# Fused decay-and-add of the samples' recurrent states, a gate chunk loaded ahead, and gate products moved between their fill sites

## What is computed

```python
def step(S, blk):                       # HGRN2, one chunk
    ...
    S = S * jnp.exp(b_last)[..., None] + jnp.einsum(
        "bhsk,bhsv->bhkv", kc * jnp.exp(b_last[:, :, None] - b), vc)
    return S, o
...
merged = (jax.nn.sigmoid(gate_a) * (o_a.astype(x.dtype) @ w_branch_a)
          + jax.nn.sigmoid(gate_b) * (o_b.astype(x.dtype) @ w_branch_b))
```

## Time and profile before

| | before |
|---|---|
| runs (3) | 1315.21, 1316.23, 1316.17 us; median 1316.17 |
| the profiled execution: its time | 1315.27 us |
| the profiled execution: its span | 1313.5 us |
| PE busy | 1284.6 us, 98% of the span |
| DVE, ACT, POOL busy | 28%, 18%, 4% |
| DMA | 449.40 MB, mean 342 GB/s |

### The profile page before, as it was taken

The page is one execution under the profiler, slowest core; times in us unless marked ns, Lnnn a source line. Parts: engine busy times, 40 slices in busy tenths (PEclk is TensorE's granted clock), DMA queues, the critical chain, the costliest instruction groups (busy, mean ns, idle before and its releaser), DMA issues.

```text
span 1313.5 us, 18378 instructions
## 1 busy us (share of the span) xinstructions
PE 1284.6 (98%) x7361; PEld 614.0 (47%) x7361; DVE 372.6 (28%) x1016; ACT 241.7 (18%) x532; POOL 56.6 (4%) x131
## 2 busy tenths in 40 slices
PE   9999999999999999999999999999999999999997
PEld 6778778888744333333333333333333333233333
DVE  3234756554327121121221211212112111211112
ACT  3144343222122110111111110111101101110102
POOL 5000200000060000000000000000000000000000
PEclk9999999999999999999999999999999999999999
DMA  7635437111879999999999999999999999999996
GB/s 237 171 99 192 132 84 271 38 33 34 311 276 380 427 430 429 428 429 428 429 428 428 430 429 431 430 429 428 430 430 430 430 430 428 430 431 429 430 428 268
DMA packets 73252, 449.40 MB, mean 342 GB/s; under 512 B 14408, under 2 KB 43130, under 8 KB 47884
## 3 DMA queue, kind: packets, MB, share of 16 engines
q1 hardware_dynamic: 67462, 445.45, 82.9%
q10 hardware_dynamic: 5734, 3.14, 0.8%
HBM read 443.82 MB, written 4.76 MB: 342 GB/s over the span
## 4 chain that ended last, share of the span: by engine, by line
PE 83%; DMA 12%; DVE 2%; ACT 2%; issue 1%; ACTq 0%; SPq 0%; DVEq 0%
PE bank L1289 27%; PE bank L1310 14%; DMA arena<-in_expert_w_gu_dram 7%; PE bank L568 7%; PE bank L1204 5%; PE bank L658 5%; DMA ring<-in_expert_w_gu_dram 5%; PE bank L1235 5%; PE bank L1082 2%; PE bank L1056 2%; PE bank L949 2%; ACT arena L1434 1%; PE bank L1211 1%; PE bank L1279 1%; PE bank L932 1%; PE bank L615 1%
## 5 line engine op out<-in xcount | busy, mean ns | idle before, releaser
L1289 PE MATMUL bank<-ring,arena 128*64 128x512 f32 x1040 | 233.6, 594 | 5.0 <-DMA ring<-in_expert_w_gu_dram 5.0
L1434 ACT ACTIVATE arena<-bank 128x512 f32<-128x512 f32 (+7 forms) x233 | 115.1, 514 | 479.2 <-PE bank L1310 196.2
L1289 PE MATMUL bank<-arena 128*64 128x512 f32 x768 | 173.3, 594 | 2.4 <-DMA arena<-in_expert_w_gu_dram 2.4
L1434 ACT ACTIVATE arena<-arena 128x256 f32<-128x256 f32 (+7 forms) x124 | 68.9, 564 | 468.6 <-DVE arena L2395 461.1
L1289 PEld LDWEIGHTS bank<-ring,arena 128*64 128x64 f32 x1040 | 72.8, 137 | 146.3 <-issue 122.6
L2395 DVE TENSOR_SCALAR arena<-bank 128x256 f32<-128x256 f32 x64 | 26.9, 421 | 375.1 <-PE bank L1289 375.1
L1310 PE MATMUL bank<-ring,arena 128*64 128x512 f32 x544 | 121.9, 595 | 0.0
L2441 DVE COPY arena<-bank 64x512 f32<-64x512 f32 x30 | 20.8, 694 | 318.5 <-PE bank L1310 318.5
L1289 PEld LDWEIGHTS bank<-arena 128*64 128x64 f32 x768 | 53.9, 137 | 105.8 <-issue 92.6
L1204 PE MATMUL bank<-arena 128*64 128x512 f32 x372 | 89.6, 599 | 0.0
L568 PE MATMUL bank<-arena,ring 128*128 128x296 f32 (+1 forms) x352 | 87.6, 411 | 0.0
(11 more groups left out here) (374 smaller groups left out, 1128.0 us busy)
## 6 DMA issues: line engine op xcount, KB each, us to landing
ring<-in_expert_w_gu_dram SPq DMA_DIRECT2D x63, 2048.0 KB, 23.3
arena<-in_expert_w_gu_dram SPq DMA_DIRECT2D x47, 2048.0 KB, 23.0
ring<-in_expert_w_down_dram SPq DMA_DIRECT2D x35, 2048.0 KB, 23.2
arena<-in_expert_w_down_dram SPq DMA_DIRECT2D x21, 2048.0 KB, 24.3
extra<-in_expert_w_gu_dram SPq DMA_DIRECT2D x15, 2048.0 KB, 25.3
ring<-in_w_in_dram SPq DMA_DIRECT2D x23, 1024.0 KB, 5.4
extra<-in_expert_w_down_dram SPq DMA_DIRECT2D x6, 2048.0 KB, 25.6
ring<-in_w_out_dram SPq DMA_DIRECT2D x4, 1024.0 KB, 7.5
```

What stands on the lines that cost most here:

```text
L1289: ins = mm(bank[q % 2][64 * (q // 2):64 * (q // 2) + 64, :], gu_lhs(c), w[:, q * 512:(q + 1) * 512], start=(c == 0), stop=(c == KT - 1), s ...
L1434: return nc.scalar.activation(out, in_, f, **kw)
```

## The change

On DVE, the decay multiply and the add become one instruction per sample and head (32 `scalar_tensor_tensor` of 128 columns in place of 8 + 8 instructions of 512), and none of it can come ahead of the product that it adds.

On PE, 3 gate products are put ahead of the wait of the samples' scores and 1 behind the scores. `gate((9, 6)[g])` in `hgrn_sample` becomes `gate((1, 10)[g])`, so that the count is 56 at the same place as before (4 more early, 4 fewer here). `bank_free` waits for the exact copy for the first two gate groups rather than for all 31 of the projections'.

On SP, gate chunk 15 is loaded into `extra` right behind chunk 14 and the HGRN2 states, and not into the ring; the load of expert 1's chunk into `extra` comes later, when PE is done with chunk 15, and before the stores of the samples' RWKV states. Chunks 16 to 19 now wait for no more than the end of the projections (16 waited for the samples' scores too, 19 for chunk 15).

```diff
@@ SP and the tables of chunks
+        AHEAD = (15,)
+        def mix_signal(n):
+            if n < N_IN + 6 and n not in AHEAD:
+                return ring_loaded[n % RING_MIX], 16 * sum(m not in AHEAD for m in range(n % RING_MIX, n + 1, RING_MIX))
+            x = n - AHEAD[0] if n in AHEAD else n - N_IN - 6
+            return wo_loaded[x], 16 if n in AHEAD or x >= len(AHEAD) else 32
...
-                if n >= RING_MIX and n < N_IN + 6:
+                if n >= RING_MIX and n < N_IN + 6 and n != 20:
                     m = n - RING_MIX
+                    if m in AHEAD:
+                        m -= RING_MIX
...
-                if n == 16:
-                    sp.wait_ge(S("smp_pe"), smp_pe["scores"] + 2)
                 if n == 20:
+                    sp.wait_ge(S("pj_done"), pj_after(AHEAD[0]))
+                    w_load(sp, 1, 10)
                     sp.wait_ge(S("smp_act"), smp_act["out"] + 4)
                     for b in range(NB):
                         src, dst = smp_state(S0T, rwkv_s, b)
                         sp.dma_start(dst, src).then_inc(S("rws_out"), 16)
+                    sp.wait_ge(S("pj_done"), pj_after(n - RING_MIX))
...
-                    w_load(sp, 1, 10)
+                    for a in AHEAD:
+                        dst, src = mix_chunk(a)
+                        sp.dma_start(dst, src).then_inc(mix_signal(a)[0], 16)
@@ PE
                 if k >= E_BLOCK:
-                    pe.wait_ge(S("pj_evac"), max(E_BLOCK, k - 1))
+                    pe.wait_ge(S("pj_evac"), k - 1 if k >= E_BLOCK + 2 else k - 2)
...
             def smp_scores():
+                gate(3)
                 pe.wait_ge(S("smp_dve"), smp_dve["ins"] + 1)
...
+                gate(1)
                 for G in range(2):
                     pe.wait_ge(S("smp_act"), smp_act["s0"] + G + 3)
...
                 for g in range(2):
-                    gate((9, 6)[g])
+                    gate((1, 10)[g])
@@ DVE
             for g in range(2):
-                for h in range(HA):
-                    a = s0v[:, 4 * g:4 * g + 4, h, :]
-                    i = v.tensor_tensor(a, a, bcast(gam[:, h, 8 + 4 * g:12 + 4 * g].unsqueeze(2), [P, 4, P]), ALU.mult)
-            step(i)
-            for g in range(2):
                 dve.wait_ge(S("hg_skv"), g + 1)
                 for h in range(HA):
-                    a = s0v[:, 4 * g:4 * g + 4, h, :]
-                    step(v.tensor_tensor(a, a, bank[4 + h].rearrange("p (b v) -> p b v", b=4), ALU.add), "hg_upd")
+                    for b in range(4):
+                        a = s0v[:, 4 * g + b, h, :]
+                        i = v.scalar_tensor_tensor(out=a, in0=a, scalar=pc(gamH, h * 16 + 8 + 4 * g + b),
+                                                   in1=bank[4 + h][:, b * P:(b + 1) * P], op0=ALU.mult, op1=ALU.add)
+                    step(i, "hg_upd")
```

More of the change, by code:

```diff
@@ L279, in layer_kernel @@
         ba, bb, wo = (w.rearrange("(k p) c -> p k c", p=P) for w in (w_branch_a[0], w_branch_b[0], w_out[0]))
+        AHEAD = (15,)
[4 more added lines that the diff above has]
+            return wo_loaded[x], 16 if n in AHEAD or x >= len(AHEAD) else 32
         def mix_chunk(n):
             s = (n + 3) % RING_MIX if n < N_IN + 6 else n - (N_IN + 6) + RING_MIX
-            slot = ring[:, s * CH:(s + 1) * CH]
+            slot = ring[:, s * CH:(s + 1) * CH] if n not in AHEAD else extra[:, (n - AHEAD[0]) * CH:(n - AHEAD[0] + 1) * CH]
             if n < N_IN:
@@ L400, in _ @@
             sp.dma_start(xn[NS:NS + NB, 2, :], state_shift[0]).then_inc(S("shift_loaded"), 16)
-            for n in list(range(EARLY)) + [N_IN + 6, N_IN + 7] + list(range(EARLY, N_IN + 6)):
+            for n in [n for n in range(EARLY) if n not in AHEAD] + [N_IN + 6, N_IN + 7] + list(range(EARLY, N_IN + 6)):
                 if n == N_IN + 6:
@@ L429, in _ @@
                         sp.dma_start(dst, src).then_inc(S("rws_out"), 16)
+                    sp.wait_ge(S("pj_done"), pj_after(n - RING_MIX))
                 dst, src = mix_chunk(n)
-                sp.dma_start(dst, src).then_inc(ring_loaded[n % RING_MIX] if n < N_IN + 6 else wo_loaded[n - N_IN - 6], 16)
+                sp.dma_start(dst, src).then_inc(mix_signal(n)[0], 16)
                 if n == 0:
@@ L531, in chunk_ready @@
             def chunk_ready(n):
[L532 to L535, removed]
+                pe.wait_ge(*mix_signal(n))
             pe.wait_ge(S("ident"), 1)
```

## The result

| | before | after | after − before |
|---|---|---|---|
| median of 15 runs each | 1315.57 us | 1318.25 us | +2.68 |
| lowest to highest | 1314.96 to 1316.3 | 1317.01 to 1321.26 | |
| profiled execution: its time | 1315.27 | 1318.25 | +2.98 |
| profiled execution: its span | 1313.5 | 1316.4 | +2.9 |

The ratio is 1.0022, with a 95% interval of 1.0015 to 1.0030. That lies at the border of what I called no change (0.2%, 2.6 us); the interval leaves no doubt of the sign, and it is the side that was forecast. The page's first part gives PE 1286.0 us busy (1284.6 before), and DVE 372.5 (372.6). The granted clock is 0.998 in the mean (0.999 before). The windows give 1.00, the upper of its two levels, up to 1310 us in both, by when the 2.9 us are there, so no clock is in this.

The account below looks back on a forecast made before the run. PE bounds the kernel early, then the experts' weight stream, which shifts with PE's delay before 400 us. +1.10 + 0.58 = +1.7 us on 1315.27 gives 1316.95, plus half of 0.90: 1317.4 us; range 1315.0 to 1319.6.

Parts of the forecast that it names:

- the two new waits: PE idles some 0.8 us for ACT ahead of the first skv and 1.85 us for DVE ahead of L801.
- the sum: +1.10 us at the samples' scores and +0.58 us at the samples' state update, together +1.7 us.
- State update: Samples' state update: each fused group takes 4.60 us, so L801 comes 0.58 us later relative to the outputs' end.
- (a): State update's waits for DVE: each fused instruction takes its whole 343 ns; +3.3 us, 1319.0 us; chance 0.14.
- (b): State update: fused instructions overlap, a group takes the additions' 2.85 us; -0.1 us, 1315.6 us; chance 0.14.
- Scores: PE around the samples' scores: 2.20 us of gate products replace 1.10 us idle, everything behind 1.10 us later.
- Rival (c): Hidden PE waits for chunk 15 and in small matmuls up to 163 us vanish; perhaps 1313 us; chance 0.05.
- Loads at nothing: SP's moved loads, chunk 15 early and expert 1's chunk later: they cost and bring nothing.
- rival (d): Chunk 15, or 16 to 19, arrive late; PE waits for DMA at first products; up to +5 us; chance 0.03.
- The chances: Whole kernel: slower by over 0.2% 0.22, within 0.72, faster 0.06; the forecast itself 0.64.
- Both engines are late by the same amount, and I see nothing that takes it back: PE behind L801 and DVE behind the state update keep their distances, so the delay carries on unchanged.
- The experts "else unchanged": Experts' chain: 1.7 us later and otherwise unchanged, with DMA in it from about 995 us.

Follow-up runs that it names:

- the repeat: The changed kernel run again with no edit, against the kernel before: median 1318.0 us against 1315.84, ratio 1.0017.
- experiment 5: The kernel before with only the changed loads and their waits, gate products and DVE instructions as before: median 1315.61 us against 1315.80, ratio 0.9996.
- experiment 4: The changed kernel with unfused decays and additions alternating by group, gate products 3 and 6, then 5: median 1314.62 us against 1315.84 before, ratio 0.9991.

## Why the prediction was right, and where it wasn't

Sign, size class and the two new waits came as forecast: +2.68 us measured in the medians (+2.2 in the repeat) where the sum said +1.7 and the forecast 1317.4 against 1318.25. But it came closer to the border than the forecast meant, for reasons that it didn't have, and in part the sum was lucky. It said 1.7 us for 200 us, where the change itself costs 1.28; L814 came at 199.77, as forecast (199.7), only because 0.48 us of start-up stood in for what the sum had too much. By its steps:

- **State update: right.** The first skv starts 1.47 us behind the outputs' end (T = 186.16 after), forecast 1.48; DVE begins at T + 2.68, as forecast; the second skv at T + 7.59 (7.60); L814 at T + 13.61 (13.54). The waits are 0.71 and 1.95 us (0.8 and 1.85). The term is +0.57 by the table (0.58). T is read from the timeline here and was read from the chain in the prediction, which puts it 0.07 us later; by the timeline alone L801 was at T + 13.03 before. The choice of 4.60 us from the row of L2090, over the addition's 2.85 and the 343 ns of the earlier trace rows, was the decisive one. Rivals (a) and (b) both fall by it: (a) read the mean of a group, 343 ns, as what one costs in a string, though the next one starts 0.26 us after it.
- **Scores: right in kind, +1.10 forecast, +0.71 measured.** Two things were missed. The old wait had a second part that showed as no idle time: scores and "stack" lay 0.88 us apart (144.97 to 145.85), while the scores now take 0.62 (145.74 to 146.36), so 0.26 us more of waiting was removed. And three products in one string moved the scores by 1.39 us (from 144.35 to 145.74), not by the 1.66 of their busy row, since matmuls overlap the modelled end of the work ahead; the fourth cost 0.68 where I had 0.54. 1.10 − 0.26 − 0.27 + 0.14 = 0.71. Rival (c) had the first of the two, hidden waits in the strings of small matmuls, but needed 4.3 us of them where 0.26 was found.
- **Loads at nothing: right**, by experiment 5, and rival (d) falls with it.
- **The chances.** The parts for "slower by over 0.2%", 0.14, 0.03 and 0.06, add up to 0.23 and not 0.22.
- **"Both engines are late by the same amount, and I see nothing that takes it back": this step failed.** The delay did not stay what it was at 200 us; it grew by 0.65 us from the two pauses of DVE, which come with 16 more instructions in its program. The prediction had itself named this test: that it is wrong if the delay at 200 us and that at the end differ. They do, 1.76 and 2.9 us. So the time was right within its range, while the account of it was short of two terms and had the scores' term 0.39 us too large, which hid part of what was missing.
- **The experts "else unchanged": wrong by 0.5 us** in the profiled execution and by 0.3 in the repeat, a term that one of the two executions with the fused instructions alone has and the other doesn't. It is not shown to belong to the change.
- **The Read-Write Bubble.** The Trainium skill's rule of large tiles ("Advanced Engine Details and Errata", section "TRN2 Errata") agrees in sign with the new kernel: 4.60 us for 16 instructions of 128 columns, against 2.85 for 4 of 512, though the 4 are plain additions, another operation. The estimate of 208 ns each from "Vector Engine (DVE) Microarchitecture Reference", section "Measured stream behaviour on trn2", does not: it is 288 ns in the mean in all the traces, and 0.26 us where no semaphore wait lies between, and the measurement decides.

## What to carry to other kernels

Fusing two instructions shortens an engine's own work, which pays where that work is on the path; if one of the two could run ahead of a wait, the fusion puts it on the path (here 3.4 us with all else unchanged, for 1.4 us of DVE saved). Ask first which half doesn't need the late operand, and lay it under the other engine's work in slices, as experiment 4 does. After an edit that changes the number of instructions of an engine on a tight path, look for short pauses between two of its own instructions far from the edit, before giving their time to the edit itself.

## What the runs showed of the hardware that I had not expected

- DVE pauses of 0.40 and 0.38 us between two of its own instructions, moved in and out by 16 memsets of 32 columns that cost nothing on the path themselves; 0.64 to 0.72 us behind each, a packet of instructions on queue 14.
- A memset of 512 columns is 0.48 us, but each that waits for the one before by a semaphore comes 0.66 us after it: the handover took 0.17 us.
- The load of expert weights near 1026 us ends, less what PE is late by at 422 us, −0.35 to +0.59 us from before's, with the same bytes and queue; two executions of one kernel, the fused instructions alone, lie 0.84 us apart.
- Fused instructions of 128 columns start 0.26 us apart in a string, and 0.38 us apart where the next waits by a semaphore for the one before.
